# RWKV stage: head sums by one product with the block of ones, no widening products, chunks written out, the small stages in later levels

## The reference

```python
kk = hs(k * k_k)
kk = kk / jnp.maximum(jnp.sqrt(jnp.sum(kk * kk, axis=-1, keepdims=True)), 1e-12)
k = k * (1.0 + (a - 1.0) * k_a)
y = wkv7(hs(r), hs(decay), hs(k), hs(v), -kk, kk * hs(a))     # the recurrence over tokens
mean = jnp.mean(y, axis=-1, keepdims=True)
var = jnp.mean(jnp.square(y - mean), axis=-1, keepdims=True)
y = ((y - mean) * lax.rsqrt(var + GN_EPS)).reshape(bn, s, rw) * ln_w + ln_b
bonus = jnp.sum(hs(r) * hs(k) * r_k, axis=-1, keepdims=True) * hs(v)
y_a = (y + bonus.reshape(bn, s, rw)) * g
```

## Time and profile before

| what | value |
|---|---|
| median of 3 runs | 2853.84 us (2852.36 to 2854.16) |
| the profiled execution's own time | 2851.79 us |
| its span | 2850.1 us |
| TensorE busy | 2673.1 us (94%) |
| VectorE, ScalarE, GpSimd busy | 1346.2, 903.1, 818.3 us |
| mean granted clock of TensorE | 0.974 |
| the RWKV stage, 318 to 790 us | TensorE 415.12 of 472.00 us busy, clock 0.93 |

### The profile page before, as it was taken

How to read it: one execution, slowest core, us unless ns; L and a number is a source line. 1 busy time by engine, 2 the same in 40 slices (tenths; PEclk the granted TensorE clock), 3 DMA queues, 4 the chain that set the end, 5 groups by cost and what they waited for, 6 DMA issues and landing times. The chain is left out here.

```text
span 2850.1 us, 37086 instructions
## 1 busy us (share of the span) xinstructions
PE 2673.1 (94%) x13827; PEld 2221.7 (78%) x13827; DVE 1346.2 (47%) x1710; ACT 903.1 (32%) x1352; POOL 818.3 (29%) x693
## 2 busy tenths in 40 slices
PE   6999699889989999989989999979999999999996
PEld 4778588778768887877777888968878888888885
DVE  5441366556434546586585445643244314421433
ACT  3442343434333322323223334322233212321322
POOL 3222323233142222263273221132222222222220
PEclk9999799999989999999999999989999999999998
DMA  2111000000012211143142124631111111111112
GB/s 85 45 44 48 15 1 1 1 1 1 1 47 56 59 44 51 42 132 118 44 156 97 46 72 154 209 100 48 48 41 52 48 48 44 52 48 48 47 45 70
DMA packets 247093, 164.63 MB, mean 58 GB/s; under 512 B 23981, under 2 KB 235463, under 8 KB 244935
## 3 DMA queue, kind: packets, MB, share of 16 engines
q1 hardware_dynamic: 245568, 162.34, 18.8%
q10 hardware_dynamic: 1415, 0.77, 0.1%
HBM read 129.51 MB, written 29.36 MB: 56 GB/s over the span
## 5 line engine op out<-in xcount | busy, mean ns | idle before, releaser
L374 POOL TENSOR_TENSOR dense_lo<-dense_raw,dense_hi 128x512 fp32r<-128x512 f32 x324 | 430.2, 1328 | 1249.8 <-ACT dense_hi L367 1248.6
L367 ACT CAST dense_hi<-dense_raw 128x512 fp32r<-128x512 f32 x324 | 192.6, 595 | 852.5 <-PE acc_o L1596 796.9
L1596 PE MATMUL acc_o<-a_hi,dense_hi 128*128 128x512 f32 x1328 | 413.3, 393 | 8.0 <-POOL a_lo L2482 4.6
L1596 PE MATMUL acc_o<-a_lo,dense_hi 128*128 128x512 f32 x1328 | 410.4, 390 | 0.0
L1596 PE MATMUL acc_o<-a_hi,dense_lo 128*128 128x512 f32 x1328 | 410.1, 390 | 0.0
L1596 PE MATMUL acc_o<-c_hi,dense_hi 128*128 128x512 f32 x1096 | 341.4, 393 | 16.9 <-POOL dense_lo L374 15.3
L1596 PE MATMUL acc_o<-c_lo,dense_hi 128*128 128x512 f32 x1096 | 339.1, 391 | 0.0
L1596 PE MATMUL acc_o<-c_hi,dense_lo 128*128 128x512 f32 x1096 | 338.6, 390 | 0.0
L1596 PEld LDWEIGHTS acc_o<-a_hi,dense_hi 128*128 128x128 f32 x1328 | 248.2, 189 | 61.2 <-POOL a_lo L2482 5.8
L1596 PEld LDWEIGHTS acc_o<-a_hi,dense_lo 128*128 128x128 f32 x1328 | 250.2, 188 | 52.4
L1596 PEld LDWEIGHTS acc_o<-a_lo,dense_hi 128*128 128x128 f32 x1328 | 250.2, 188 | 52.3
(11 more groups left out here) (380 smaller groups left out, 3796.5 us busy)
## 6 DMA issues: line engine op xcount, KB each, us to landing
dense_raw<-in_f_w_up SPq DMA_DIRECT2D x176, 256.0 KB, 2.9
dense_raw<-in_f_w_down SPq DMA_DIRECT2D x72, 256.0 KB, 2.8
w_raw_e<-in_e_w_in SPq DMA_DIRECT2D x44, 256.0 KB, 2.9
s_states<-t_hx SPq DMA_DIRECT2D x16, 512.0 KB, 3.5
g_in<-s_inputs SPq DMA_DIRECT2D x8, 1024.0 KB, 5.1
hx<-s_states SPq DMA_DIRECT2D x8, 1024.0 KB, 5.0
dense_raw<-in_o_w_glu SPq DMA_DIRECT2D x32, 256.0 KB, 2.8
s_inputs<-t_in SPq DMA_DIRECT2D x14, 512.0 KB, 3.2
```

What stands on the lines that cost most here:

```text
L367: nc.scalar.copy(self.hi[:, par, 0:n, :], self.raw[:, par, 0:n, :]).then_inc(w_hi_done, 1)
L374: pool.tensor_tensor(self.lo[:, par, 0:n, :], self.raw[:, par, 0:n, :], self.hi[:, par, 0:n, :].bitcast(F32), op=ALU.subtract).then_inc(w_ ...
L1596: last = nc.tensor.matmul(acc[:, h * HALF:(h + 1) * HALF], w[:, chunk, j, :], x[:, k + j, h * HALF:(h + 1) * HALF], start=first, stop=final)
```

## The change

head_sums becomes one product of 128x512 with head_ones (128x128, ones within a head), as the bonus already has it: each channel then holds its head's sum. The tile norms grows from 8 partitions x 2 x 128 to 128 partitions x 2 x 4 x 128, the floors and roots work on it, and zr_dve and gn_dve read it from SBUF instead of PSUM. The eight widening products (two calls of four) and the construction of head_in and head_out go. The small stages move: the head sums of k from ahead of level 0 to level 1, behind the gate; centring from between level 0 and grow 1 to level 2; the sum for y from level 2 to 3; on VectorE level0_dve ahead of biased_dve, the floor of k into level 1, that of y into level 3, gn_dve into level 5; on ScalarE the sigmoids behind level 0, centred_act into level 2, the roots into level 3, all exponentials into level 4. The loop of turns 1 to 6 is written out.

```diff
-        norms = sb(sc, "norms", [HEADS, 2, CH])
+        norms = sb(sc, "norms", [P, 2, RT, CH])
         def head_sums(bank, sq):
-            for i in range(RT):
-                last = nc.tensor.matmul(bank[0:HEADS, 0:CH], head_in[:, i, :], sq[:, i, :], start=i == 0, stop=i == RT - 1)
-            return last
-        def widen(bank, by_head):
-            return product4(bank, lambda i: head_out[:, i, :], lambda i: by_head[:, :])
+            return nc.tensor.matmul(bank[:, :], head_ones[:, :], sq, start=True, stop=True)
-        def k_wide_pe(pe, c):
-            wait(pe, "roots", c, 2)
-            wait(pe, "gn", c, back=2)
-            up(widen(prep_ps[1], norms[:, 0, :]), "k_wide")
-        def y_wide_pe(pe, c):
-            wait(pe, "roots", c + 2, 2)
-            up(widen(prep_ps[1], norms[:, 1, :]), "y_wide")
         def floor_dve(dve, c):
             wait(dve, "k_sum", c)
-            wait(dve, "k_wide", c, back=1)
-            up(nc.vector.tensor_scalar(norms[:, 0, :], prep_ps[1][0:HEADS, 0:CH], 1e-24, None, ALU.max), "k_floor")
+            wait(dve, "kk", c, back=1)
+            up(nc.vector.tensor_scalar(norms[:, 0, :, :], psum4(prep_ps[1]), 1e-24, None, ALU.max), "k_floor")
         def zr_dve(dve, c, s):
-            wait(dve, "k_wide", c)
-            up(tt(T["kk"], T["kk"], psum4(prep_ps[1]), ALU.mult), "kk")
+            wait(dve, "roots", c, 2)
+            up(tt(T["kk"], T["kk"], norms[:, 0, :, :], ALU.mult), "kk")
         def gn_dve(dve, c):
-            wait(dve, "y_wide", c)
-            up(tt(y_c[:, :, :], y_c[:, :, :], psum4(prep_ps[1]), ALU.mult), "gn")
+            wait(dve, "roots", c + 2, 2)
+            up(tt(y_c[:, :, :], y_c[:, :, :], norms[:, 1, :, :], ALU.mult), "gn")
@@ turn_of_pe
                 lora_codes_pe(pe, c + 1)
-                k_sum_pe(pe, c + 1)
             level0_pe(pe, c)
-            if late:
-                centre_pe(pe, c - 1)
             for k in range(1, LEVELS):
                 grow_pe(pe, c, k)
                 if more and k == 1:
                     lora_gate_pe(pe, c + 1)
+                    k_sum_pe(pe, c + 1)
                 if late and k == 2:
+                    centre_pe(pe, c - 1)
+                if late and k == 3:
                     y_sum_pe(pe, c - 1)
-                if late and k == 4:
-                    y_wide_pe(pe, c - 1)
-                if more and k == 5:
-                    k_wide_pe(pe, c + 1)
@@ turn_of_act
-            if more:
-                sigmoids_act(act, c + 1)
             for k in range(LEVELS):
                 level_act(act, c, k)
-                if late and k == 0:
-                    centred_act(act, c - 1)
-                if k == 2:
+                if more and k == 0:
+                    sigmoids_act(act, c + 1)
+                if late and k == 2:
+                    centred_act(act, c - 1, not more)
+                if more and k == 2:
+                    gate_act(act, c + 1)
+                if k == 3:
                     if more:
-                        gate_act(act, c + 1)
                         roots_act(act, c + 1, 0, 2 if late else 1)
...
-                if more and k == 3:
+                if more and k == 4:
                     exps_act(act, c + 1, 1 - s, 0)
-                if more and k == 4:
                     exps_act(act, c + 1, 1 - s, 1)
@@ turn_of_dve
             scores_dve(dve, c)
+            level0_dve(dve, c)
             if more:
                 biased_dve(dve, c + 1)
-                floor_dve(dve, c + 1)
-            level0_dve(dve, c)
             for k in range(1, LEVELS):
                 mask_dve(dve, c, k)
                 if more and k == 1:
+                    floor_dve(dve, c + 1)
                     logsum_dve(dve, c + 1)
-                if k == 2:
+                if more and k == 2:
+                    k2_dve(dve, c + 1)
+                if k == 3:
                     if late:
                         y_floor_dve(dve, c - 1)
-                    if more:
-                        k2_dve(dve, c + 1)
-                if k == 3:
                     mid_state_dve(dve, c, s)
-                if late and k == 4:
+                if late and k == 5:
                     gn_dve(dve, c - 1)
@@ all_turns
-            turn_of(eng, 0, 0, True, False)
-            with eng.Fori(0, NCH // 2 - 1) as n:
-                for k in (1, 2):
-                    turn_of(eng, n * 2 + k, k % 2, True, True)
-            turn_of(eng, NCH - 1, 1, False, True)
+            for c in range(NCH):
+                turn_of(eng, c, c % 2, c < last_chunk, c > 0)
```

More of the change, by code:

```diff
@@ L777, in trunk @@
         y_c = sb(sc, "y_c", [P, RT, CH])
-        head_in = sb(sc, "head_in", [P, RT, HEADS])
-        head_out = sb(sc, "head_out", [HEADS, RT, P])
         state = sb(sc, "state", [P, RT, HEAD])
@@ L792, in trunk @@
                     "a_zb": 2, "x0": 7, "xt0": 6, "res0": 1, "akv": 2, "sa": 2, "y": 1, "y_sq": 2},
-            "pe": {"lora": 3, "k_sum": 1, "k_wide": 1, "bonus_sum": 1, "turned": 3, "a_ps": 8, "mx_ps0": 6, "mx_ps1": 6,
+            "pe": {"lora": 3, "k_sum": 1, "bonus_sum": 1, "turned": 3, "a_ps": 8, "mx_ps0": 6, "mx_ps1": 6,
                    "x_ps0": 13, "x_ps1": 13, "res_ps0": 2, "res_ps1": 2, "akv_ps": 1, "sa_ps": 2, "s_ps": 1,
-                   "y_ps": 1, "yc_ps": 1, "y_sum": 1, "y_wide": 1},
+                   "y_ps": 1, "yc_ps": 1, "y_sum": 1},
             "dve": {"biased": 2, "logsum": 4, "mids": 1, "k2": 2, "k_floor": 1, "y_floor": 1, "kk": 1, "zr": 2,
@@ L873, in centre_pe @@
             if isinstance(c, int) and c == last_chunk:
-                wait(pe, "gn", c, back=1)
+                wait(pe, "y_floor", c, back=1)
             elif isinstance(c, int) and c == last_chunk - 1:
@@ L1104, in roots_act @@
         def roots_act(act, c, first=0, n=2):
-            tile_ = norms[:, first:first + n, :]
+            tile_ = norms[:, first:first + n, :, :]
             if first == 0:
@@ L1112, in roots_act @@
             wait(act, "roots", c, 1)
-            up(nc.scalar.activation(tile_, tile_, ACT.Exp, scale=-0.5, bias=unscale[0:HEADS, 0:1]), "roots")
+            up(nc.scalar.activation(tile_, tile_, ACT.Exp, scale=-0.5, bias=unscale[:, 0:1]), "roots")
         def centred_act(act, c, last=False):
@@ L1192, in floor_dve @@
             wait(dve, "k_sum", c)
-            wait(dve, "k_wide", c, back=1)
-            up(nc.vector.tensor_scalar(norms[:, 0, :], prep_ps[1][0:HEADS, 0:CH], 1e-24, None, ALU.max), "k_floor")
+            wait(dve, "kk", c, back=1)
+            up(nc.vector.tensor_scalar(norms[:, 0, :, :], psum4(prep_ps[1]), 1e-24, None, ALU.max), "k_floor")
         def y_floor_dve(dve, c):
             wait(dve, "y_sum", c)
-            wait(dve, "y_wide", c, back=1)
-            up(nc.vector.tensor_scalar(norms[:, 1, :], prep_ps[1][0:HEADS, 0:CH], 1.0 / HEAD, GN_EPS,
+            wait(dve, "gn", c, back=1)
+            up(nc.vector.tensor_scalar(norms[:, 1, :, :], psum4(prep_ps[1]), 1.0 / HEAD, GN_EPS,
                                        ALU.mult, ALU.add), "y_floor")
         def zr_dve(dve, c, s):
-            wait(dve, "k_wide", c)
-            up(tt(T["kk"], T["kk"], psum4(prep_ps[1]), ALU.mult), "kk")
+            wait(dve, "roots", c, 2)
+            up(tt(T["kk"], T["kk"], norms[:, 0, :, :], ALU.mult), "kk")
             wait(dve, "kk", c)
@@ L1452, in all_turns @@
         def all_turns(eng, turn_of):
-            turn_of(eng, 0, 0, True, False)
-            with eng.Fori(0, NCH // 2 - 1) as n:
-                for k in (1, 2):
-                    turn_of(eng, n * 2 + k, k % 2, True, True)
-            turn_of(eng, NCH - 1, 1, False, True)
-        lora_loaded, r_consts, eyes, selectors = sem("lora_loaded"), sem("r_consts"), sem("r_eyes"), sem("r_selectors")
+            for c in range(NCH):
+                turn_of(eng, c, c % 2, c < last_chunk, c > 0)
+        lora_loaded, r_consts, eyes = sem("lora_loaded"), sem("r_consts"), sem("r_eyes")
         with nc.Block() as block:
@@ L1508, in _ @@
                 start(pool, "pool")
[L1509 to L1520, removed]
                 raw_pool(pool, 0)
@@ L1535, in _ @@
                 pe.wait_ge(eyes, 4)
-                pe.wait_ge(selectors, 2 + RT + 3)
                 lora_codes_pe(pe, 0)
@@ L1540, in _ @@
                 bonus_pe(pe, 0)
-                k_wide_pe(pe, 0)
                 turn_pe(pe, 0, 0, B_TOK)
@@ L1546, in _ @@
                 y_sum_pe(pe, last_chunk)
-                y_wide_pe(pe, last_chunk)
     def at(name, shape, where, dt=F32):
```

## The result

The changed kernel took 2815.2 us (median of 4 runs, 2811.9 to 2815.8) against 2854.0 (2852.4 to 2856.5) of the kernel before on the same chip: ratio 0.9863, 95% interval 0.9851 to 0.9876. Predicted were 2815.5. Its profiled execution took 2815.83, span 2814.1.

A forecast was written before the change was run, and what follows sets the result against it. TensorE, busy some 50 of every 54 us in the RWKV stage, was taken as the bound. Savings of 20.2 + 5.7 + 0.7 + 1.55 + 1.15 + 9.0 = 38.3 us gave 2813.5 profiled, 2815.5 as median; range 2803 to 2829.

The forecast's parts named there:

- step 1: TensorE's stop before the head sums of k, between codes and grow 1: 5.5 us saved in chunk 2.
- Levels 1 to 3: VectorE free of the scans at 463.4, grow 2 ending at 464.7 and grow 4 at 473.25 in chunk 2.
- step 4: Ln and Exp over 128x1024 delay ScalarE's copy of level 4, so grow 5 starts about 1.1 us late.
- step 5: Level 5: VectorE's gn and zr held up by GpSimd; 3.4 us saved per middle chunk, 20.2 in six.
- The rival without contention: VectorE and GpSimd don't hold each other up in level 5: 4.9 us saved a chunk, 2806 us; chance 0.20.
- The rival with the longer chain: VectorE and ScalarE late in levels 1, 4, 5, plus semaphore hops: 1.5 us more a middle chunk, 2824.5; chance 0.14.
- steps 6 and 7: Chunk 0 gains 5.7 us, chunk 7 0.7; removing the uncovered widening at the two ends gains 1.55 and 1.15.
- step 8: The loop's two jumps cost 4.69 and 4.31 us; writing the turns out saves 9.0.
- The rival in which the gaps stay: The jump was not the cause and gaps stay in the written-out chunks: 9.0 us less gain, 2824.5; chance 0.12.
- the slower one: TensorE's sequencer can't get straight code in time: gaps of 4.7 us, two a turn giving 2890 us; chance 0.04.

The follow-up runs named there:

- GpSimd's order: The changed kernel with GpSimd doing b_pool ahead of out_pool: 2810.6 us, ratio 0.9865 to the kernel before.
- the form alone: The kernel before, loop included, with the new head_sums, norms and roots and no widening, every stage in its old place: 2862.8 us, ratio 1.0036.
- the kernel with gn in the refinement: The changed kernel with gn_dve moved from level 5 into the refinement and b_pool ahead of out_pool: 2807.6 us, ratio 0.9845.

## Why the prediction was right

The time, the direction and the mechanism of each step were right. That the time came out within 0.3 us was luck: two sizes were off, each more than that, and against each other. So it is taken step by step, on the profiled executions (36.0 us less, where 38.3 were predicted; the stage 41.3 less).

1. *The stop (step 1).* Right in mechanism and size: codes to gate 9.46 and then 3.82, 5.6 saved for 5.5. The old stop was 2.8 of waiting. The rest was the slow clock behind it, the narrow products and the centring in the queue; what each of these is worth was not measured apart.
2. *Levels 1 to 3.* Right: the scans freed VectorE at 451.19 (451.35 expected, in this kernel's time 12.05 earlier).
3. *The roots (step 4).* Right: grow 5 at 465.21, 465.25 expected, a wait of 0.90. Halving them gave 0.87 a chunk back, so the cause is shown.
4. *Level 5 (step 5).* Mechanism right, size 0.55 too dear: refinement at 474.70, 475.25 expected; the chunk gained 3.9, not 3.4. I let gn wait 0.52 where it waited 0.3, and zr's block ended earlier: VectorE's sums came at 470.17 for 470.70. Six chunks: 23.4 for 20.2. The rival without contention (4.9) is refuted by GpSimd's order, which moved zr from 1.42 to 0.69 and the whole stage by 4.5. The rival with the longer chain (1.5 more a chunk than 50.8) is refuted by the chunks of 50.3. One reading in step 5 was loose: the copy in level 6 did not end 0.55 after GpSimd's operation as zr did, but with it (490.13 and 490.11).
5. *Chunks 0 and 7, the ends (steps 6 and 7).* Chunk 0 gained 5.7 for 5.7 (by the 3.93 from codes to grow 1 of step 1 it should have read 5.6); the preparation took 24.04 and then 22.58, 1.46 for 1.55; from the last chunk's start to the next stage 59.86 and then 58.17, 1.69 for 1.85.
6. *The loop (step 8).* The excess of the four long chunks, 9.0, is gone. But 9.0 was the price of the two jumps in the kernel before only: with the loop in the changed kernel the stage is 12.5 longer (its gaps are 4.0), and written out alone, in the kernel before, the stage of one execution was 12.7 shorter (3.0 of it by two short chunks), the median 7.1. The rival in which the gaps stay is out; so is the slower one, for no turn of the straight code shows a gap.
7. *What I left out: the rest of the kernel.* I put it at nothing, and behind the stage it took 6.3 us longer in the pair of profiles, 5.3 in the second pair. Against it stood 3.2 more in the six chunks and a start of the stage that came 1.0 earlier. So the profiled execution gained 36.0 for 38.3. In the medians beside it, where the kernel before was slower than in its profile, the gain was 38.8, and 37.6 when both were run again; part of the close hit is this spread.

What the three parts are worth, by the stage of one profile each: the form alone costs 4.9 (472.3 to 477.2), moving the small stages then gains 33.6 (477.2 to 443.6, with the loop), writing out gains 12.5. By the medians, which hold the rest of the kernel too, it is 10.8, 31.8 and about 16. The two counts differ because executions of the kernels with the stop and the loop vary: the stage of the kernel before was 470.1 in its second profile, and those with the form alone took 2855.7 to 2869.3. The order and the rough sizes are shown, single microseconds are not. The moved stages with the old narrow sums were not tried, so it is not shown that the new form is needed for the gain.

## What to carry to other kernels

A small operation ahead of the critical step in an in-order queue costs more than itself: its wait, and here in most chunks the slow clock behind the wait. Put it where the bound engine waits anyway; a single wide product cost 0.12 in such a place, where four narrow ones took 1.03 of TensorE behind the old stop. Before a PSUM operand is replaced by one in SBUF, or an activation widened, look at what GpSimd runs beside it and how much slack the next copy has. Both prices (0.3 for gn and 0.7 for zr; 0.9 for the roots) could be estimated from the trace before, and reordering took away zr's and the roots' and moved gn to where TensorE does not wait for it.

## What the runs showed of the hardware that was not expected

- The same 2.85 us stop is followed by a fallen clock in some chunks and by the full one in others: 54.2 or 52.7 us a chunk. A wait of 1.67 us is followed by either as well (2.49 or 1.60 for the same dozen of products). This goes with the wide spread of the kernel before (2844 to 2857 us) beside 2812 to 2816 of the changed one.
- The gap at a loop's jump is not fixed: 2.6 to 3.1 us in the two profiles of the kernel before, 3.7 and 3.8 with the new form alone, 4.0 in the changed kernel with its loop.
- A copy of 128x4 on VectorE (end_scale) took 1.25 us beside a GpSimd operation in the changed kernel, and 0.16 with GpSimd idle in the kernel with gn in the refinement.
